# Expert weights inside the hidden activations, and a tail whose gathers add into SBUF

## The reference

```python
def hier_moe(h, ...):                        # 4 groups of 4 experts, experts are SwiGLU of width 256
    gi = argmax(t @ w_group);  gw = softmax(t @ w_group)[gi]
    tv, ti = top_k(router logits of group gi, 2)
    tw = softmax(tv) * gw                    # two weights for each token
    for e in range(16):
        he = silu(t @ w_exp_gate[e]) * (t @ w_exp_up[e])
        out = out + dense_w[:, e:e + 1] * (he @ w_exp_down[e])
x = x + hier_moe(rmsnorm(x, norm_ffn))
y = rmsnorm(x, norm_final)
```

## Time and profile before

| | |
|---|---|
| median of three executions | 930.65 us |
| the profiled execution, its own time | 931.3 us |
| its span, first to last instruction | 929.5 us |
| PE, DVE, ACT, POOL: busy share of the span | 91%, 50%, 42%, 20% |
| DMA bytes | 142.46 MB, 153 GB/s over the span |

### The profile page before, as it was taken

How to read it: one execution, slowest core, us unless ns; L and a number is a source line. 1 busy time by engine, 2 the same in 40 slices (tenths; PEclk the granted TensorE clock), 3 DMA queues, 4 the chain that set the end, 5 groups by cost and what they waited for, 6 DMA issues and landing times.

```text
span 929.5 us, 13492 instructions
## 1 busy us (share of the span) xinstructions
PE 842.9 (91%) x5122; PEld 720.3 (77%) x5122; DVE 464.3 (50%) x760; ACT 392.1 (42%) x540; POOL 190.2 (20%) x131
## 2 busy tenths in 40 slices
PE   4999999999999999999999999999988989899910
PEld 3988878988788888887888888888977878788700
DVE  4411354454428642323231436613598778777537
ACT  4522244444432533334424212314445667678413
POOL 0001010100000001100100000400003777687553
PEclk9999999999999999999999999999999999999965
DMA  9214131322221312240311211792859999988675
GB/s 290 82 46 113 64 73 47 74 57 37 54 71 46 91 46 31 76 109 10 65 46 47 91 45 47 226 401 106 294 203 332 364 372 379 392 293 294 226 274 216
DMA packets 97263, 142.46 MB, mean 153 GB/s; under 512 B 4508, under 2 KB 75372, under 8 KB 97164
## 3 DMA queue, kind: packets, MB, share of 16 engines
q1 hardware_dynamic: 89276, 115.04, 37.0%
q0 software_dynamic: 7904, 26.44, 10.4%
q10 hardware_dynamic: 32, 0.26, 0.3%
HBM read 116.31 MB, written 25.43 MB: 152 GB/s over the span
## 4 chain that ended last, share of the span: by engine, by line
PE 77%; DVE 8%; DMA 4%; ACT 4%; SPq 4%; issue 3%; POOL 1%; ACTq 0%; DVEq 0%; POOLq 0%
PE main L828 20%; PE main L830 20%; PE main L829 20%; PE work L865 2%; PE work L895 2%; PE work L928 2%; PE work L912 2%; SPq L578 2%; ACT prob_t L1208 1%; PE work L882 1%; PE work L1084 1%; DVE x L1873 1%; PE work L1031 1%; DMA raw<-in_w_in 1%; DMA e_raw<-in_w_exp_down 1%
## 5 line engine op out<-in xcount | busy, mean ns | idle before, releaser
L1444 DVE TENSOR_TENSOR w_lo<-raw,w_hi 128x2048 fp32r<-128x2048 f32 x30 | 68.7, 2290 | 260.0 <-ACT w_hi L1152 260.0
L828 PE MATMUL main<-ht_hi,w_hi 128*128 128x512 f32 (+1 forms) x576 | 197.1, 342 | 0.0
L829 PE MATMUL main<-ht_lo,w_hi 128*128 128x512 f32 (+1 forms) x576 | 193.9, 337 | 0.0
L830 PE MATMUL main<-ht_hi,w_lo 128*128 128x512 f32 (+1 forms) x576 | 193.8, 336 | 0.0
L828 PEld LDWEIGHTS main<-ht_hi,w_hi 128*128 128x128 f32 x576 | 109.2, 190 | 18.8 <-issue 4.7
L830 PEld LDWEIGHTS main<-ht_hi,w_lo 128*128 128x128 f32 x576 | 109.2, 190 | 11.8
L829 PEld LDWEIGHTS main<-ht_lo,w_hi 128*128 128x128 f32 x576 | 109.3, 190 | 11.6
L678 POOL DMA_DIRECT2D bias<-bias_vectors x16 | 12.4, 774 | 427.2 <-DVE nmx L1504 183.6
L828 PE MATMUL main<-w_hi,ht_hi 128*128 128x256 f32 (+1 forms) x304 | 96.3, 317 | 3.4 <-DVE ht_lo L1461 3.4
L829 PE MATMUL main<-w_lo,ht_hi 128*128 128x256 f32 (+1 forms) x304 | 93.9, 309 | 0.0
L830 PE MATMUL main<-w_hi,ht_lo 128*128 128x256 f32 (+1 forms) x304 | 93.9, 309 | 0.0
(11 more groups left out here) (265 smaller groups left out, 1531.3 us busy)
## 6 DMA issues: line engine op xcount, KB each, us to landing
e_raw<-in_w_exp_gate SPq DMA_DIRECT2D x16, 1024.0 KB, 8.3
e_raw<-in_w_exp_up SPq DMA_DIRECT2D x16, 1024.0 KB
e_raw<-in_w_exp_down SPq DMA_DIRECT2D x16, 1024.0 KB
raw<-in_w_in SPq DMA_DIRECT2D x28, 512.0 KB, 4.6
expert_rows<-y_sb SPq DMA_DIRECT2D x19, 512.0 KB, 9.0
raw<-in_w_in SPq DMA_DIRECT2D x9, 1024.0 KB, 5.3
expert_rows<-y_sb SPq DMA_DIRECT2D x1, 5632.0 KB, 22.7
raw<-in_w_out SPq DMA_DIRECT2D x4, 1024.0 KB, 5.3
```

What stands on the lines that cost most here:

```text
L828: pe.matmul(out, s_hi, m_hi, start=(first and i == 0), stop=False)
L829: pe.matmul(out, s_hi, m_lo, start=False, stop=False)
L830: last = pe.matmul(out, s_lo, m_hi, start=False, stop=(final and i == n - 1))
L1444: dve.tensor_tensor(w_lo[:, c % 2, :], raw[:, c % 2, :], w_hi[:, c % 2, :], ALU.subtract).then_inc(s_wlo, 1)
```

## The change

It does four things. (1) The one-hot tables move to memory that stays free until tile 0, and DVE makes a third table there, `hot_weight` (the tile's one-hot times the token's weight); PE multiplies it with `hot_slot` between gate_up(0) and turn_hidden(0) (`weight_table`), which gives `weights`, the routing weight of every row of every tile (times 0.5). (2) In each tile DVE copies the tile's column of `weights` to `weight_column`, and the second pass of `hidden` multiplies with it where it had 0.5. So the rows in `y_dram` carry their weights. (3) In the tail each gather is an indirect DMA with an addition: it adds the expert rows to `x1` in SBUF. First the six of k = 0, each behind the load of its x1 tile, then the six of k = 1, each behind the one of k = 0. The additions and scalings on DVE, ACT and POOL are gone, and `yg` too. (4) SP stores tile 2 of the last tiles before it loads x1 back; ACT loads the table of the square root before the tail, and squares t + 1 before it takes the root of t.

The hunk that renames the semaphores is left out.

```diff
--- before.py
+++ after.py
@@ -107,16 +107,6 @@
 DIL_K = [[9, 11, 1], [3, 5, 7]]
 GATE_A = [0, 2, 4, 6, 12, 14, 8, 10]
 GATE_B = [b + 1 for b in GATE_A]
-
-
-SHARED = 3
-
-
-def combined(t):
-
-    return 2 * (t + 1) - max(0, t + 1 - SHARED)
-
-
 
 
 HALVES = [("vd", pair, i) for pair in range(2) for i in range(2)]
...
@@ -333,6 +323,8 @@
         resets = at("resets", [P, E, NT], F32, A_S + 7456)
         table_u = at("table_u", [P, TILES_PAD], U32, A_S + 8576)
         column = at("column", [P, 2], U32, A_S + 8960)
+        weights = at("weights", [P, TILES_PAD], F32, A_S + 6528)
+        weight_column = at("weight_column", [P, 2], F32, A_S + 6688)
         fl = at("fl", [P, 2, NT], F32, A_S + 8704)
         wt = at("wt", [P, 2, NT], F32, A_S + 8768)
         both = at("both", [P, 2, NT, E], F32, A_BLK + 24576 + 20480)
...
@@ -340,10 +332,10 @@
         gain3 = at("gain3", [P, D], F32, A_S + 8992)
         assert A_S + 8992 + 4096 <= A_END
 
-        hot_slot = at("hot_slot", [P, 2, NT, P], F32R, A_BLK + 24576 + 12288)
-        hot_tile = at("hot_tile", [P, 2, NT, TILES_PAD], F32R, A_BLK + 24576 + 18432)
-
-        yg = at("yg", [P, NT, 2, D], F32, A_HT)
+        hot_slot = at("hot_slot", [P, 2, NT, P], F32R, A_OA + 24576)
+        hot_tile = at("hot_tile", [P, 2, NT, TILES_PAD], F32R, A_OA + 24576 + 6144)
+        hot_weight = at("hot_weight", [P, 2, NT, TILES_PAD], F32, A_EH + 4096)
+
         junk3 = at("junk3", [P, D], F32, A_HT + 49152)
 
 
...
@@ -636,12 +629,13 @@
             load_tile(loops, 4, (2,))
             store_y(loops, 1)
 
+            store_y(loops, 2)
             for c in range(3):
                 sp.wait_ge(s_elo[c], loops * 2 + 4)
                 sp.nop()
             for t in range(NT):
-                sp.dma_start(x1[:, t, :], x1_dram.ap()[P * t:P * t + P, :]).then_inc(s_x1back, 16)
-            for j in range(2, 5):
+                sp.dma_start(x1[:, t, :], x1_dram.ap()[P * t:P * t + P, :]).then_inc(s_x1back[t], 16)
+            for j in range(3, 5):
                 store_y(loops, j)
             sp.wait_ge(s_yout[0], loops * 16 + 16 * 3)
             sp.sem_inc(s_ystored, 1)
...
@@ -763,14 +757,15 @@
             split_lo_part(loops, 4, 2)
 
             gp.wait_ge(s_ystored, 2)
-            for t in range(NT):
-                for k in range(2):
-                    gp.indirect_dma_start(yg[:, t, k, :], None, y_dram.ap(),
-                                          bass.IndirectOffsetOnAxis(ap=slots_u[:, 0, k, t:t + 1], axis=0)).then_inc(s_yg[t], 16)
-            gp.wait_ge(s_x1back, 16 * NT)
-            for t in range(SHARED, NT):
-                gp.wait_ge(s_scaled, t - SHARED + 1)
-                gp.tensor_tensor(x1[:, t, :], x1[:, t, :], yg[:, t, 0, :], ALU.add).then_inc(s_added, 1)
+            for k in range(2):
+                for t in range(NT):
+                    if k == 0:
+                        gp.wait_ge(s_x1back[t], 16)
+                    else:
+                        gp.wait_ge(s_yg[t], 16)
+                    gp.indirect_dma_start(x1[:, t, :], None, y_dram.ap(),
+                                          bass.IndirectOffsetOnAxis(ap=slots_u[:, 0, k, t:t + 1], axis=0),
+                                          compute_op=ALU.add).then_inc(s_yg[t], 16)
 
 
         @block.tensor
...
@@ -1117,9 +1112,20 @@
                                                     (hi[:, k, cols], lo[:, k, cols])) for k in range(2)])
                 last.then_inc(s_dn, 1)
 
+            def weight_table():
+
+                pe.wait_ge(s_hotw, 2)
+                for i in range(2 * NT):
+                    k, t = divmod(i, NT)
+                    last = pe.matmul(main[1][:, 512 + TILES_PAD:512 + 2 * TILES_PAD], hot_slot[:, k, t, :].bitcast(F32),
+                                     hot_weight[:, k, t, :], start=(i == 0), stop=(i == 2 * NT - 1))
+                last.then_inc(s_wtable, 1)
+
             def tile(r, j):
                 turn_rows(r, j + 1)
                 gate_up(r, j)
+                if not late(r, j, 1):
+                    weight_table()
                 if late(r, j, 1):
                     down(r, j - 1)
                 turn_hidden(r, j)
...
@@ -1415,18 +1421,22 @@
             tanh_gate(loops, 4)
             hidden_hi(loops, 4)
 
+            def square3(t):
+                act.wait_ge(s_yg[t], 32)
+                if t >= 1:
+                    act.wait_ge(s_sq3, t)
+                act.activation(junk3[:, :], x1[:, t, :], ACT.Square, accum_out=ss[:, 2, t:t + 1]).then_inc(s_sq3, 1)
+
+            def root3(t):
+                act.wait_ge(s_v3, 2 * (t + 1))
+                act.activation(ss[:, 2, t:t + 1], ss[:, 2, t:t + 1], ACT.Sqrt).then_inc(s_root3, 1)
+
+            act.activation(lams[:, 0:1], eps[:, :], ACT.Sqrt)
+            square3(0)
             for t in range(NT):
-                act.wait_ge(s_comb, combined(t))
-                if t >= 1:
-                    act.wait_ge(s_ss3, 2 * t)
-                act.activation(junk3[:, :], x1[:, t, :], ACT.Square, accum_out=ss[:, 2, t:t + 1]).then_inc(s_ss3, 1)
-                if SHARED <= t + 2 < NT:
-
-                    act.wait_ge(s_yg[t + 2], 32)
-                    act.activation(yg[:, t + 2, 0, :], yg[:, t + 2, 0, :], ACT.Copy,
-                                   scale=wt[:, 0, t + 2:t + 3]).then_inc(s_scaled, 1)
-                act.wait_ge(s_v3, 2 * (t + 1))
-                act.activation(ss[:, 2, t:t + 1], ss[:, 2, t:t + 1], ACT.Sqrt).then_inc(s_ss3, 1)
+                if t + 1 < NT:
+                    square3(t + 1)
+                root3(t)
 
 
         @block.vector
...
@@ -1751,6 +1761,7 @@
                 rt(dve.tensor_reduce(value(6), four(7), AX.X, ALU.max))
                 dve.tensor_tensor(value(4), value(6), value(2), ALU.subtract).then_inc(s_diffs, 1)
 
+            dve.wait_ge(s_fill, 16)
             for k in range(2):
                 rt_on(dve.tensor_tensor(hot_tile[:, k, :, :], over(slots_f[:, 1, k, :], [P, NT, TILES_PAD], 2),
                                         over(small[:, C_IOTA:C_IOTA + TILES_PAD], [P, NT, TILES_PAD], 1), ALU.is_equal))
...
@@ -1785,6 +1796,13 @@
                 rt(dve.reciprocal(value(11), value(10)))
                 rt(dve.tensor_tensor(wt[:, 0, :], value(11), value(9), ALU.mult))
                 rt(dve.tensor_tensor(wt[:, 1, :], wt[:, 0, :], value(5), ALU.mult))
+                for k in range(2):
+                    rt(dve.tensor_tensor(hot_weight[:, k, :, :], over(slots_f[:, 1, k, :], [P, NT, TILES_PAD], 2),
+                                         over(small[:, C_IOTA:C_IOTA + TILES_PAD], [P, NT, TILES_PAD], 1), ALU.is_equal))
+                    dve.tensor_tensor(hot_weight[:, k, :, :], hot_weight[:, k, :, :],
+                                      over(wt[:, k, :], [P, NT, TILES_PAD], 2), ALU.mult).then_inc(s_hotw, 1)
+                dve.wait_ge(s_wtable, 1)
+                rt(dve.tensor_scalar(weights[:, :], main[1][:, 512 + TILES_PAD:512 + 2 * TILES_PAD], 0.5, None, ALU.mult))
 
 
             def rows_lo(r, j):
...
@@ -1802,14 +1820,18 @@
 
             def hidden(r, j):
 
+                par = j % 2
+                column_j = bass.ds(r * 2 + j, 1) if late(r, j, 3) else slice(j, j + 1)
+                dve.tensor_copy(weight_column[:, par:par + 1], weights[:, column_j]).then_inc(s_wcol, 1)
                 dve.wait_ge(s_tanh, r * 2 + (j + 1))
                 if late(r, j, 2):
                     dve.wait_ge(s_htr, r * 2 + (j - 1))
-                par = j % 2
                 ps = main[0][:, 512 * par:512 * par + 512]
                 dve.scalar_tensor_tensor(he[:, par, :], tanh_g[:, par, :], 1.0, ps[:, 0:DE], ALU.add, ALU.mult).then_inc(s_he, 1)
                 dve.wait_ge(s_he, r * 4 + (2 * j + 1))
-                dve.scalar_tensor_tensor(he[:, par, :], he[:, par, :], 0.5, ps[:, DE:2 * DE], ALU.mult, ALU.mult).then_inc(s_he, 1)
+                dve.wait_ge(s_wcol, r * 2 + (j + 1))
+                dve.scalar_tensor_tensor(he[:, par, :], he[:, par, :], weight_column[:, par:par + 1], ps[:, DE:2 * DE],
+                                         ALU.mult, ALU.mult).then_inc(s_he, 1)
 
             def hidden_lo(r, j):
                 dve.wait_ge(s_hehi, r * 2 + (j + 1))
...
@@ -1855,27 +1877,16 @@
 
             def finish(t):
                 r = ss[:, 2, t:t + 1]
-                dve.wait_ge(s_ss3, 2 * t + 1)
+                dve.wait_ge(s_sq3, t + 1)
                 dve.tensor_scalar(r, r, 1.0 / D, EPS, ALU.mult, ALU.add).then_inc(s_v3, 1)
                 dve.wait_ge(s_v3, 2 * t + 1)
                 dve.reciprocal(r, r).then_inc(s_v3, 1)
-                dve.wait_ge(s_ss3, 2 * t + 2)
+                dve.wait_ge(s_root3, t + 1)
                 dve.scalar_tensor_tensor(x1[:, t, :], x1[:, t, :], r, gain3[:, :], ALU.mult, ALU.mult).then_inc(s_y3, 1)
 
             dve.wait_ge(s_gain3, 16)
-            dve.wait_ge(s_x1back, 16 * NT)
             for t in range(NT):
-                dve.wait_ge(s_yg[t], 32)
 ```

(22 more changed lines are left out.)

## The result

The changed kernel takes **943.18 us** (median of four executions, 942.72 to 943.54) against 930.55 us before (median of four, one more than the three above): a ratio of 1.0128, 95% interval [1.0111, 1.0146]. It is slower, by 12.6 us where the forecast had 10.6. The profiled execution has a span of 941.6 us, 12.1 more than before.

The account below looks back on a forecast made before the run. It took the chain of waits as the bound, touched at tile 0 and in the tail (DMA-bound gathers, then additions and norm). Tile 0 +4.0, stream +14.6, after it -8.0 make +10.6: 930.65 to 941 us; range 924 to 948 us.

Parts of the forecast that it names:

- Tile 0: what is added.: Between gate_up(0) and the transposes: DVE passes 1.4 us, PE products 2.5 us, small steps and waits; about 4.4 us in all.
- Is it lost to the end?: Tile 0's delay passes on to the end: 4.0 us lost, 0.4 us taken up by loads; ends 0 and 4.5 us.
- a sign against it: Tile 0's delay gone by 797 us would show the forecast wrong.
- Each tile.: A 128x1 column copy on DVE per tile, 0.15 us, hidden in DVE's idle time; second hidden pass unchanged; no cost.
- The rule on copies that was set against it: Trainium skill: SBUF-to-SBUF copies and GpSimd can shut each other out, so the column copy would wait for POOL's split.
- The way into the tail.: SP's x1 loads start 1.9 us later, behind tile 2's store, and land at 887.7 us: hidden by 3.7 us.
- The tail: what comes.: Twelve adding gathers at 2.6 us each, reading two operands, lengthen the DMA stream by 14.6 us.
- a danger to the forecast: A mean POOL issue well over 1 us in the tail would move the bound from the DMA engines to POOL.
- The tail: what goes.: After the last gather 7.7 us remain in place of 15.7 us: 8.0 us less.
- A free addition: Tail: the second read overlaps the first, gathers stay at 1.33 to 1.47 us, time 926 us; chance 0.28.
- a draw: Tail gathers at 1.56 to 1.87 us; gain and loss nearly cancel, within 1.86 us of 930.65 us; chance 0.11.
- One after the other: Tail: x1 reads can't overlap the next row, 3.2 to 5 us per gather, time 948 to 970 us; chance 0.07.

Follow-up runs that it names:

- the first try of the early weights: Changed kernel with the weight table made before tile 0 and the tile numbers moved to the weights' old place: 941.68 us, ratio 1.0112.
- early weights with both in every tile: Changed kernel with the table made among PE's idle products before tile 0, tile numbers left in place, column and second pass kept: 937.37 us, ratio 1.0066.
- half rows: Changed kernel with gathers that add only the first 2 KB of each 4 KB row: 934.59 us, ratio 1.0043.

## Why the prediction was right

**Tile 0: what is added.** Right in kind, a little short: 5.05 us at the transposes against 4.4 worked out. DVE's four passes were 0.36 us each, as their row had it. PE's table was 3.14 us against 2.5, and that is the gap. In the first try of the early weights the same 24 products took 2.76 us at a granted clock of 1.00 (from 692.02 us on); the other 0.4 us go with the clock that fell within them.

**Is it lost to the end?** Here the step failed. "I let 0.4 us be taken up and take 4.0": 5.9 us were lost, outside the ends of 0 and 4.5. The prediction had nothing of the clock. At the lower level the eight turnings of rows (1.92 us in place of 1.04) and the first products of the next tile (0.43 us apart in place of 0.23) took longer too, and that tile's products were done about 7.3 us later than before: 5.05 us at the transposes and 2.3 us behind them. The loads did take something back, about 1.4 us, so the thought of a buffer was right and its size too small; but the share of 0.00 from 712 to 714 us shows that the store was empty by then. The delay was not gone by 797 us, which the prediction had named as a sign against it: it was 5.98 us there. The experiments show that the place of the table makes the loss; how it divides between the wait and the clock they don't.

**Each tile.** Right: sixteen copies of a column took a mean of 143 ns and the first three 146. Sixteen of the nineteen ran while POOL was in a split, and none was held up. The second pass did change, to 0.48 us from 0.42, where the prediction had it unchanged, but early weights with both in every tile cost nothing that could be measured. The rule on copies that was set against it did not bite at this shape; it is the 128x608 pass with two inputs from SBUF that was held.

**The way into the tail.** Right in effect, with a later start: the loads of x1 were issued at 881.70 us, 8.1 us later than before, 5.9 of it from ahead. They took 3.46 us to issue and a median of 7.4 us to land, and the gathers at 897.30 us waited for SP's signal that the rows were stored, as before.

**The tail: what comes.** Right: 2.51 us for a gather against 2.6, and 14.4 us more of stream against 14.6. The ground for it, that an addition reads two operands, was the right choice between ends of 1.33 and 5 us, and the same gathers without the addition bear out the factor; the two reads themselves are not seen, and half rows suggest that the bytes are not all of it, so the step is better shown in its sum than in its reason. The DMA engines didn't run dry (share 1.04 to 1.07). POOL's issues grew to 1.84 us apart, which had been named as a danger to the forecast; below 2.51 us it stayed hidden.

**The tail: what goes.** Right: 8.2 us against 8.0.

**The sum.** The span grew by 12.1 us where 10.6 were forecast. Tile 0 was 1.9 us worse than taken, and the tail 0.4 us better; no large errors cancelled.

**The rivals.** A free addition needed less than 1.56 us for a gather, a draw less than 1.87; 2.51 us excludes both. One after the other (3.2 us and more) did not come either.

## What to carry to other kernels

An addition that is taken from an engine and given to a DMA is not gone: in a stretch in which the DMA engines are full it costs about as much as a second transfer, here 1.24 us more for 512 KB (2.51 less 1.27), against 1.24 us on a DVE that may have had the time (2.49 us for two). Giving the DMA only two or three of the twelve made a shorter tail, 35.7 to 36.0 us against 38.1 before and 37.2 with all of them on DVE, but the time of the kernel does not tell the two apart. And a small serial step in front of a busy TensorE can cost more than its length: here 5.9 us to the end for 5.05 us at the transposes, with loads that ran dry and a clock that fell behind it. The same step some 13 us earlier, where PE makes idle products anyway, cost nothing that could be measured.

## What was not expected of the hardware

- An adding gather costs POOL 1.54 us to issue (for 512 KB and for 256 KB), a plain one 0.94 us in the kernel that differs by the addition alone.
- The granted clock fell from 1.00 to 0.50 within 24 narrow products (128x32), with PE idle for 2.36 us or for only 0.59 us before them; it did not fall in tile 0 of the kernel before, where PE waited 1.83 us without such products, nor behind the same 24 products when they stood among idle ones at 694 us, where the clock had been at 0.50 and rose to 1.00 as they began. In the first try of the early weights it fell to 0.50 as well, within a wait of 4.07 us and without such products. What sets it off stays open.
- A 128x608 pass on DVE with two inputs from SBUF took 4.27 us in place of 0.78 beside POOL's split; the 128x1 copies never were held, sixteen of them beside such a split.
